# Last mixers: block heads ahead of the differential heads, the differential norm behind the second maxima, forgetting heads' norm together with the latents'

## The reference

```
h = rms_norm(x) @ w_in                       # 2916 columns
cq, ckv, kr, fox_qkv, fox_f, moba_qkv, diff_qkv, mem_q = split(h)
o_a = latent attention (cq, ckv normed, then @ mla_w_uq, mla_w_ukv; 4 heads of 96, rope)
o_b = forgetting attention (q, k normed by head; scores + cumulated log_sigmoid(fox_f + b))
o_c = block attention (q, k normed by head, rope on 16; one block at this length: causal)
o_d = softmax(q1 k1) v - lam * softmax(q2 k2) v      # q, k normed by head of 32, rope on 8
o_d = rms_norm(o_d, sub_norm) * (1 - lam_init)
o_e = attention over 256 memory tokens (q, k normed)
x = x + concat(o_a, o_b, o_c, o_d, o_e) @ w_o
```

## Time and profile before

| | |
|---|---|
| median of 3 runs | 1487.51 us (1485.81 to 1489.91) |
| the profiled execution | 1490.72 us, its span 1489.4 us |
| TensorE busy | 1443.7 us (97%) |
| VectorE, ScalarE busy | 993.7 us (67%), 774.1 us (52%) |
| attention of the last mixers, layer 0 | 821.96 to 921.17 us of the span |
| the same, layer 1 | 1180.55 to 1279.18 us of the span |

### The profile page before, as it was taken

One profiled execution on the slowest core, in us unless ns is written; L12 is line 12 of the kernel. 1 busy time (PEld: TensorE's weight loads), 2 busy tenths in 40 slices (PEclk: granted clock), 3 DMA queues, 4 the chain that ended last, 5 costly groups with the idle time before them and its releaser, 6 DMA issues.

```text
span 1489.4 us, 26045 instructions
## 1 busy us (share of the span) xinstructions
PE 1443.7 (97%) x10884; PEld 1371.8 (92%) x10884; DVE 993.7 (67%) x1495; ACT 774.1 (52%) x1219; POOL 110.9 (7%) x100
## 2 busy tenths in 40 slices
PE   7999989999999989999999999999999998999999
PEld 7989989999997989999997889999998787999999
DVE  5566667655589767654586766877756676677763
ACT  6654444444475544443376765544445685644442
POOL 0004211100000011100000000011100000011100
PEclk9999999999999999999999989999999998999999
DMA  8531246555463345655554312555565321355553
GB/s 261 151 129 58 86 142 198 179 190 181 159 223 121 110 137 179 191 178 194 175 168 130 125 57 86 189 176 181 179 202 181 133 86 57 112 175 187 179 177 107
DMA packets 186573, 228.19 MB, mean 153 GB/s; under 512 B 5964, under 2 KB 161228, under 8 KB 186456
## 3 DMA queue, kind: packets, MB, share of 16 engines
q1 hardware_dynamic: 185448, 221.75, 46.5%
q0 software_dynamic: 1008, 4.77, 0.9%
HBM read 225.46 MB, written 1.05 MB: 152 GB/s over the span
## 4 chain that ended last, share of the span: by engine, by line
PE 72%; DVE 17%; ACT 7%; issue 3%; POOL 0%; DMA 0%; ACTq 0%; DVEq 0%; SPq 0%; POOLq 0%
PE bank L495 20%; PE bank L497 20%; PE bank L496 19%; DVE weights_low L786 7%; ACT weights_high L684 3%; PE bank L503 3%; PE bank L1006 2%; DVE cv L2950 2%; ACT S L2143 2%; PE bank L2056 2%; PE bank L2077 2%; DVE cv L2947 1%; DVE pad L2937 1%; DVE S L2205 1%; DVE cv L2956 1%
## 5 line engine op out<-in xcount | busy, mean ns | idle before, releaser
L786 DVE TENSOR_TENSOR weights_low<-weights_raw,weights_high 128x1024 fp32r<-128x1024 f32 (+2 forms) x421 | 507.3, 1226 | 280.1 <-ACT weights_high L684 279.9
L684 ACT CAST weights_high<-weights_raw 128x1024 fp32r<-128x1024 f32 (+2 forms) x421 | 425.1, 1031 | 261.8 <-PE bank L497 260.1
L495 PE MATMUL bank<-hT_high,weights_high 128*128 128x256 f32 x1640 | 472.8, 288 | 10.1 <-DVE hT_low L862 4.9
L496 PE MATMUL bank<-hT_low,weights_high 128*128 128x256 f32 x1640 | 468.1, 285 | 0.0
L497 PE MATMUL bank<-hT_high,weights_low 128*128 128x256 f32 x1640 | 467.8, 285 | 0.0
L495 PEld LDWEIGHTS bank<-hT_high,weights_high 128*128 128x128 f32 x1640 | 317.9, 194 | 15.6 <-issue 9.1
L496 PEld LDWEIGHTS bank<-hT_low,weights_high 128*128 128x128 f32 x1640 | 317.9, 194 | 0.2
L497 PEld LDWEIGHTS bank<-hT_high,weights_low 128*128 128x128 f32 x1640 | 317.8, 194 | 0.2
L495 PE MATMUL bank<-aT_high,weights_high 128*128 128x256 f32 x864 | 242.8, 281 | 0.1
L496 PE MATMUL bank<-aT_low,weights_high 128*128 128x256 f32 x864 | 241.7, 280 | 0.0
L497 PE MATMUL bank<-aT_high,weights_low 128*128 128x256 f32 x864 | 241.5, 280 | 0.0
(11 more groups left out here) (417 smaller groups left out, 1815.0 us busy)
## 6 DMA issues: line engine op xcount, KB each, us to landing
weights_raw<-in_w_up SPq DMA_DIRECT2D x32, 1024.0 KB, 5.4
weights_raw<-in_w_down SPq DMA_DIRECT2D x32, 1024.0 KB, 5.1
weights_raw<-in_ffn_w_gate SPq DMA_DIRECT2D x22, 1024.0 KB, 5.3
weights_raw<-in_ffn_w_up SPq DMA_DIRECT2D x22, 1024.0 KB, 5.3
weights_raw<-in_w_in SPq DMA_DIRECT2D x20, 1024.0 KB, 5.1
weights_raw<-in_w_in_ab SPq DMA_DIRECT2D x16, 1024.0 KB, 5.8
weights_raw<-in_ffn_w_down SPq DMA_DIRECT2D x16, 1024.0 KB, 5.2
weights_raw<-in_w_o SPq DMA_DIRECT2D x10, 1024.0 KB, 5.0
```

Source lines behind the costliest of these rows:

```text
L495: k.E.matmul(out, xh, wh, start=first, stop=False)
L496: k.E.matmul(out, xh, wl, start=False, stop=False)
L684: k.A.copy(w.halves(n)[0], w.raw_part(n)).then_inc(*k.s.weight_high(n))
L786: k.V.tensor_tensor(low, w.raw_part(n), high.bitcast(F32), ALU.subtract).then_inc(*k.s.weight_low(n))
```

## The change

The order of the groups becomes fox, mla, moba, the two diff groups, mem, and `OUT_2`, the order of the output panels, follows. `late` is no longer used. The forgetting heads' squares, root and norm join those of the latents, behind panel 512. The block heads are normed in VectorE's third piece of `last_columns`, where the diff heads were. The diff heads' sums and means go into the fourth piece, behind the maxima of group 1 and ahead of a split; their root goes behind ScalarE's exponentials of group 1, and norm and rope go to VectorE's `amid(3)`. The root of the memory queries goes to the end of group 2, the root of the differential result to the end of group 4. In the diff below, a line that is only "..." stands for context left out.

```diff
...
 HEADS_2 = ["fox", "mla", "moba", "diff", "mem", "cq"]
-OUT_2 = [2, 0, 6, 4, 8]
+OUT_2 = [2, 0, 4, 6, 8]
...
         Group(8, 96, lambda hh: (hh, 0, 96), 96 ** -0.5, True, lambda hh, u: m.kva[:, u, hh * P + 64:(hh + 1) * P], out(1), mask=cneg, gains=heads_2(k, l, "mla")),
+        Group(4, P, in_pairs, 64 ** -0.5, True, values(C_MOBA + 512), out(2), mask=cneg, gains=heads_2(k, l, "moba")),
         Group(4, P, in_fours(0), 32 ** -0.5, True, values(C_DIFF + 512), None, mask=cneg, gains=heads_2(k, l, "diff")),
-        Group(4, P, in_fours(1), 32 ** -0.5, True, values(C_DIFF + 512), out(2), mask=cneg, shared=True),
-        Group(4, P, in_pairs, 64 ** -0.5, True, values(C_MOBA + 512), out(3), mask=cneg, gains=heads_2(k, l, "moba")),
+        Group(4, P, in_fours(1), 32 ** -0.5, True, values(C_DIFF + 512), out(3), mask=cneg, shared=True),
         Group(4, P, in_pairs, 64 ** -0.5, False, lambda hh, u: kvm[:, u, 256 + hh * 64:256 + (hh + 1) * 64], out(4), gains=heads_2(k, l, "mem"),
...
     ]
-    return Attention(("m2", l), m, groups, 2, ("o_2", l), m.out, copies_by_scalar=True, late=(1,))
+    return Attention(("m2", l), m, groups, 2, ("o_2", l), m.out, copies_by_scalar=True)
...
 def projected_to(k, l, end):
...
         lambda c, t: (qa4 if c < 4 else ka4)[:, t, c % 4, :],
+        lambda c, t: m.hp[:, t, C_MOBA + c * P:C_MOBA + (c + 1) * P],
         lambda c, t: m.hp[:, t, C_DIFF + c * P:C_DIFF + (c + 1) * P],
         None,
-        lambda c, t: m.hp[:, t, C_MOBA + c * P:C_MOBA + (c + 1) * P],
         lambda c, t: m.hp[:, t, C_MEM + c * P:C_MEM + (c + 1) * P] if c < 2 else kvm[:, t, (c - 2) * P:(c - 1) * P],
...
         elif n == 2:
+            E.wait_ge(*s.turned.at((l, "moba", 1)))
+            for mark in projected_to(k, l, 2048):
+                E.wait_ge(*mark)
+        elif n == 3:
             E.wait_ge(*s.turned.at((l, "diff", 1)))
-        elif n == 4:
-            E.wait_ge(*s.turned.at((l, "moba", 1)))
-            for mark in projected_to(k, l, D_IN2):
+            for mark in projected_to(k, l, 2560):
                 E.wait_ge(*mark)
...
     projected(512)
-    roots("cq", 0, 3)
+    squared_columns("fox", C_FOX, 512)
+    roots("cq", 0, 11)
     projected(1024)
-    squared_columns("fox", C_FOX, 512)
     latent = heads_2(k, l, "cq")
...
     A.activation(m.lf, m.lf, ACT.Ln, bias=1.0).then_inc(*s.logs((st, "ln")))
-    roots("fox", 3, 8)
     projected(1536)
...
         yield
+        scalar_split(k, n2 + 4)
+        yield
         roots("diff", SLOT["diff"], 16)
-        scalar_split(k, n2 + 4)
-        yield
         scalar_split(k, n5 + 1)
...
     def finish(n):
-        if n == 3:
+        if n == 2:
             roots("memq", SLOT["memq"], 4)
+        elif n == 4:
             scalar_root(k, (st, "sub"), m.st2[:, :, 0:4])
...
-    def scaled(*kinds, meanwhile=lambda: None):
-        first, end = SLOT[kinds[0][3]], SLOT[kinds[-1][3]] + kinds[-1][1]
+    def slots(*kinds):
+        return SLOT[kinds[0][3]], SLOT[kinds[-1][3]] + kinds[-1][1]
+
+    def scale_means(*kinds):
+        first, end = slots(*kinds)
+        means(kinds[0][3], m.st[:, :, first:end], spread(k.const("inv_d")[:, first:end], 1, NT))
+
+    def scaled(*kinds):
+        first, end = slots(*kinds)
         name, x = kinds[0][3], m.st[:, :, first:end]
-        means(name, x, spread(k.const("inv_d")[:, first:end], 1, NT))
-        meanwhile()
         vector_inverse(k, (st, name), x)
...
     projected(512)
-    scaled(*LOW_RANK)
+    squared(FOX)
+    scale_means(*LOW_RANK, FOX)
+    scaled(*LOW_RANK, FOX)
     projected(1024)
...
     V.tensor_reduce(m.lm[:, 64:66], lm3, AXX, ALU.add).then_inc(*s.lam((l, "sums")))
-    squared(FOX)
     V.wait_ge(*s.logs.at((st, "ln")))
     V.scalar_tensor_tensor(m.lf, m.fx, 0.0, m.lf, ALU.min, ALU.subtract).then_inc(*s.forget((l, "lf")))
-    scaled(FOX)
     V.wait_ge(*s.forget.last())
...
         yield
+        normed("moba", m.hp[:, :, C_MOBA:C_MOBA + 512], 8, m.st2[:, :, 12:20], 2 * ROT_M)
+        turned_heads("moba", C_MOBA, 8, 64, ROT_M, ROT_C + ROT_A)
+        vector_split(k, n2 + 2)
+        yield
         squared(DIFF)
-        scaled(DIFF, meanwhile=lambda: vector_split(k, n2 + 2))
-        turned_heads("diff", C_DIFF, 16, 32, ROT_D, ROT_C + ROT_A + ROT_M)
+        scale_means(DIFF)
         vector_split(k, n2 + 4)
-        yield
         yield
...
     def amid(step):
-        if step == 4:
-            normed("moba", m.hp[:, :, C_MOBA:C_MOBA + 512], 8, m.st2[:, :, 12:20], 2 * ROT_M)
-            turned_heads("moba", C_MOBA, 8, 64, ROT_M, ROT_C + ROT_A)
+        if step == 3:
+            scaled(DIFF)
+            turned_heads("diff", C_DIFF, 16, 32, ROT_D, ROT_C + ROT_A + ROT_M)
+        elif step == 4:
             vector_split(k, k.w.first(("in_2", l, 0, 2560)) + 4)
...
     def work(n):
...
             V.wait_ge(*s.products.at(((st, "out T", before), "T", 0)))
-        if n == 2:
+        if n == 3:
+            vector_inverse(k, (st, "memq"), queries)
             for hh in range(4):
...
             vector_scaled(k, m.d1, bank, rden, k.banks.read(key))
-        elif n == 3:
+        elif n == 4:
             vector_scaled(k, m.d2, bank, rden, k.banks.read(key))
...
             V.wait_ge(*s.lam.at((l, "minus")))
-            V.wait_ge(*k.banks.was_read((st, "values", 2)))
+            V.wait_ge(*k.banks.was_read((st, "values", 3)))
             then(V.scalar_tensor_tensor(m.d1, m.d2, m.lm[:, 66:67], m.d1, ALU.mult, ALU.add))
...
             means("sub", m.st2[:, :, 0:4], 1.0 / 64)
-            vector_inverse(k, (st, "memq"), queries)
             vector_inverse(k, (st, "sub"), m.st2[:, :, 0:4])
...
             then(last)
-            V.scalar_tensor_tensor(a.groups[3].out[0], m.d1, 1.0 - lam_init, spread(row("sub"), 1, NT), ALU.mult, ALU.mult
-                                   ).then_inc(*s.mixed((st, 3)))
+            V.scalar_tensor_tensor(a.groups[4].out[0], m.d1, 1.0 - lam_init, spread(row("sub"), 1, NT), ALU.mult, ALU.mult
+                                   ).then_inc(*s.mixed((st, 4)))
         else:
...
```

More of the change, by code:

```diff
@@ L2600, in last_columns @@
         yield
-        roots("diff", SLOT["diff"], 16)
         scalar_split(k, n2 + 4)
         yield
+        roots("diff", SLOT["diff"], 16)
         scalar_split(k, n5 + 1)
```

## The result

The changed kernel takes 1493.35 us (median of 11 runs, 1488.84 to 1498.66); the kernel before, run beside it, 1488.18 (11 runs, 1482.54 to 1490.74). The ratio is 1.0034, with a 95% interval of 1.0022 to 1.0046: slower by 5.1 us, where 1.5 us less was forecast. The profiled execution took 1496.95 us (span 1495.7), 6.2 more than the one of before; it is the second slowest of its eleven, so what its trace gives for the low clock may lie above what a middling execution pays.

The account below looks back on a forecast made before the run. TensorE, busy 97% of the span, bounds the kernel. Per layer 85.0 us work + 9.65 waits + 3.5 low clock = 98.15, 1.05 and 0.5 less than before: -1.5 us, so 1486.0 from 1487.51, range 1480.5 to 1493.5.

Parts of the forecast that it names:

- c, the low clock: Attention stretch, per layer: time lost to TensorE's lowered clock, forecast 3.5 us, from 1.4 at the end and 2.1 earlier.
- the 1.4 for the fall behind the last wait: Behind the wait for the normed differential result: a clock fall with small matmuls behind it, costing 1.4 us per layer.
- the slower rival: Clock falls at the wait for the split and stays low through values, transposes and scores, at 5.5 us; chance 0.17.
- the 85.0 us of work: Attention stretch, each layer: TensorE's work at the upper clock level, without waits or low clock, unchanged by the change.
- For the low weights: First half of the attention: TensorE waits 2.0 us for a half of weights that VectorE splits late.
- The 1.3 and 0.9 of part 2: First half of the attention: waits of 1.3 us for the block heads' exponentials and 0.9 for copied diff queries and keys.
- the 0.25 of part 3: With no product deferred: scores 4 wait 0.25 us for the values before them, only four banks being free.
- The differential result: At the fifth output: TensorE waits 4.15 us for the normed result of the diff heads, with nothing else to do.
- Part 1: Projections: the forgetting heads' norm joins the latents', worth 0; without the cover it would cost up to 3.5 us per layer.
- The one by part 1: Rival: without four halves of lead in the weight casts, TensorE waits 3.5 us in each layer: 1493 us; chance 0.04.
- The one by the wait for the split: Rival: 2.0 us standstill for split weights, then 5.5 us low clock, 1.4 at the end: 1492.7 us; chance 0.17.
- stays low for more than 10 us a layer: Sign that the forecast is wrong: TensorE's clock stays at its lower level for more than 10 us a layer.

Follow-up runs that it names:

- a_fill: Changed kernel with 36 more transposes of a constant by TensorE ahead of its wait for the normed differential result: 1482.71 us, ratio 0.9955.
- a_behind: Changed kernel with 36 more transposes of a constant behind the wait for the normed differential result, standstill kept: 1495.12 us, ratio 1.0047.
- a_early: Changed kernel with the differential norm's scaling and rope on VectorE one piece earlier, behind the third preparation: 1487.2 us, ratio 0.9999.
- a_fox: Changed kernel with the forgetting heads' squares, sums and root behind their own panel again: 1496.65 us, ratio 1.0043.
- a_fill12: Changed kernel with 12 more transposes of a constant ahead of the wait for the normed differential result: 1490.9 us, ratio 1.0014.
- a_nosub: Changed kernel with the norm of the differential heads' result left out, so that output differs: 1479.44 us, ratio 0.9941.
- a_split: Changed kernel with VectorE's split of the next weights' panel ahead of the differential norm's squares and sums: 1496.97 us, ratio 1.0054.
- a_cover: Changed kernel with the block heads' output product deferred behind the second differential group's values, to cover the differential result's norm: 1474.57 us, ratio 0.9905.

## Why the prediction was wrong

**The step that failed** is the size of c, the low clock, in the sum, and of its parts the 1.4 for the fall behind the last wait. The place was right ("I count a fall there"), the size was not. In the profiled executions it measured 5.7 and 4.9 us (13.00 and 12.17 against 7.29 and 7.30 in a_fill). The argument for 1.4 was "small matmuls behind it", taken from the second fall of before, 3.4 us long. But behind that fall stood eight transposes and scores, then a product. Behind this one stand four transposes and 32 value matmuls, and the clock stayed down through all of these and into product 4. a_behind shows that what stands there matters: with 36 transposes behind the same standstill the fall cost 1.7. The long fall of before, which I had kept for the slower rival, also had values behind it, and was the nearer row. The whole of c gives the same warning: my 3.5 lay below the 6.9 and 4.9 us that the two layers of before paid by my own figures, though I forecast more waiting than they had. (The first fall of before lasts 13.7 us by these windows, not 13.3; nothing hangs on it.)

**The sum, recomputed.** With the 85.0 us of work, layer 0 after is 103.43 = 85.0 + 9.5 + 8.9, and layer 1 is 98.86 = 85.0 + 9.5 + 4.4. The low clock reaches past the stretch: product 4 up to the next transposes took 5.40 and 4.58 us where it took 3.32 before. So c was 8.9 + 2.1 = 11.0 and 4.4 + 1.3 = 5.7, in the mean 8.3 against my 3.5. For both layers that is 16.7 - 7.0 = 9.7 us more, of which the last falls are 5.7 + 4.9 - 2.8 = 7.8 and the middle ones the other 1.9. By my figure the profiled execution would have taken 1489.2; with 9.7 more, and 0.3 less of waits, it would be 1498.6. It took 1496.95, so the rest of the span was shorter by 1.6. Against the kernel before, by the same figures, the two layers paid 3.0 us more in waits and 4.9 more in low clock, less the same 1.6: the 6.2 between the two profiled executions, to 0.1. The measured time lies just inside the range that I gave, at its slow end; the direction and the 1.5 us less were wrong.

**The waits** came as forecast in sum: 9.5 against 9.65.
- For the low weights: 2.06 against 2.0, in place.
- The 1.3 and 0.9 of part 2 and the 0.25 of part 3 did not come as waits for exponentials, queries and a bank of scores, but as one of 1.94 us, 2.45 forecast. The second values wait for a bank that VectorE frees with the last columns, and VectorE had the differential norm and the maxima in front of it. So this sum was right in part by luck. a_early takes the wait away by moving that norm.
- The fourth transpose bank: 1.25 against 0.75. The differential result: 3.95 against 4.15.
- The waits of 2.04, 1.84 and 1.79 us of before are gone, as forecast.

TensorE's timeline in the first half of layer 0, the two waits:

```profile
849.57 0.43 PE L495 MATMUL bank<-weights_high,hT_high 128*128 128x356 f32 x1 [2.06 <-DVE weights_low L786]
...
863.36 2.96 PE L2077 MATMUL bank<-kva,PT 128*128 128x64 f32 x20 [1.94 <-DVE hp L2680]
```

**Part 1** at 0 held (a_fox). **The table loads** held as read from the earlier trace rows. ScalarE's timeline behind the last copy:

```profile
913.67 0.58 ACT L2160 COPY PT<-bank 128x512 f32<-128x512 f32 x1 [1.16 <-PE bank L503]
914.27 1.28 ACT L716 ACT_TABLE_LOAD   x1
915.56 0.21 ACT L716 ACTIVATE st<-st 128x8 f32<-128x8 f32 x1
```

The load begins 0.02 us behind the copy, the root starts as it ends, and VectorE's mean is ready at 915.36, so it is all but hidden. The Trainium skill, "ScalarE: Activation LUTs", section "What ACT_TABLE_LOAD costs", has 1.38 us of drain beside each load; this trace shows none here either, and the measurement decides.

**Of the rivals**, the two slower ones came near in number, 1492.7 and 1493. The one by part 1 falls with a_fox and with the waits, which show nothing of it. The one by the wait for the split had the mechanism by halves. It put the long low clock behind the wait for the split and the short one at the end; the trace has the long one at the end in both layers, and behind the split's wait the clock held in that execution. In the profiled executions of a_early, a_fox and a_fill12 it did fall there, for 10.2 us in layer 0, so that half of the rival is real at times. Its own threshold, c over 6.5, was passed with 8.3. The prediction's list of what would show it wrong names the sign that came: a clock that "stays low for more than 10 us a layer". It came with 27.4 and 17.2; but the kernel before had 17.1 and 10.2 already, so the sign was a weak one.

**What remains open.** The middle's fall varied, 13.7 us in layer 0 and 3.4 in layer 1 of one execution, 3.4 and 13.7 in a_nosub's, with the same instructions and the same waits up to there; and in a_nosub the short one stood at 848 to 852, behind the wait for the weights. The Trainium skill, "TensorE: Matmul & The Clock Gate", section "What's actually happening", calls the number of slow matmuls run-variable in one and the same kernel, and says it of a kernel's start. These traces show the same in the middle of one. It was not tried to bring it down, and nor was the upper group of a_split's executions profiled.

## What to carry to other kernels

Before an order of work is changed, list which long chain on VectorE or ScalarE each product of TensorE covers. When the cover goes, count the wait, and then count the matmuls behind it, and the first of the next product, as if they ran at 1.2 GHz. Here that was 4.9 to 5.7 us behind a wait of 3.95 us. Behind the waits of about 2 us in the middle it varied from one layer and one execution to the next, from no fall to one of 13.7 us. If the wait can't be covered, dummy work in it gives back the clock alone (11.8 us in a_fill); real work deferred into it pays the wait as well (19.2 in a_cover).

## What the runs showed of the hardware

- The low clock behind one standstill of 3.95 us cost more than the standstill itself, 5.7 and 4.9 us in the two layers. It is counted as busy time: the page's busy total rose by 3.1 us with the same 10884 matmuls.
- The cost hangs on what follows too: 1.7 us with 36 transposes of 128x128 behind the same standstill, 4.9 to 5.7 with four of them and 32 matmuls of 64 columns.
- Standstills of 3.95, 2.7, 1.3 us and none gave ratios of 1.0034, 1.0014, 0.9971 and 0.9955, and 13.7, 10.2, 0 and 0 us of lowered clock at that place in the profiled executions. The intervals of the first two overlap, and so do those of the last two; between 2.7 and 1.3 us they do not.
